# A layer norm's division and its shift moved from VectorE into TensorE's transposing products, and one tile's squares taken by halves

## The chip, the cores and the metric

The kernel runs on one core of a Trainium2 chip. The metric is the time of one execution in microseconds (us), and lower is better. The engines are named as in the profile: PE is TensorE (PEld its weight loads), DVE is VectorE, ACT is ScalarE, POOL is GpSimd, SP is SyncE, which here only issues DMAs.

## The reference, cut to what matters

Two transformer blocks run one after the other over 256 rows of 1024 floats. The change lies in the second block, between its attention and its feed-forward part:

```
def layer_norm(x, g, b):
    mu = jnp.mean(x, axis=-1, keepdims=True)
    var = jnp.mean(jnp.square(x - mu), axis=-1, keepdims=True)
    return (x - mu) * lax.rsqrt(var + LN_EPS) * g + b

def second_block(x, ...):
    mix = token_mixer(x, w_in, b_forget, rel_bias, w_out)        # ends in y @ w_out
    x = layer_norm(DEEPNORM_ALPHA * x + mix, ln1_g, ln1_b)       # the norm that is changed
    ffn = conv_ffn(x, w_up, conv_w, conv_b, w_down)              # begins with x @ w_up
    return layer_norm(DEEPNORM_ALPHA * x + ffn, ln2_g, ln2_b)
```

The norm is thus wanted twice: turned round (features on the partitions) as the input of the product with `w_up`, and multiplied by alpha, with rows on the partitions, for the sum behind the feed-forward part.

## The kernel before, in words

The 256 rows are two tiles (`tt` 0 and 1) of 128 rows on the partitions, and the 1024 features of a row are handled in two halves of 512. Every engine has its own program, written out by hand in one order, and engines wait for each other by semaphores; `wait_ge(made, ...)` waits for a step of DVE, `acted` of ACT, `done` of PE.

The stage around the change, with the lines of the profile:

1. The second output projection `out2` (L2223) adds the groups `("mix2", tt, half)` in four PSUM banks. The last of them to be ready is tile 1's second half.
2. For each tile DVE adds the projection to `xt` and sums the rows (`row_sum`, L1573, by halves), makes minus the mean (`row_mean`, L1581), and subtracts it and multiplies by the gain (`row_centre`, L1586) into `xg[4]`.
3. ACT squares the centred rows and sums them (`centred_squares`, L962), and takes the root (`row_root`, L632). DVE takes the reciprocal (`row_rstd`, L1129) and then writes the normed rows by halves, `xg * rstd + shift` (`row_normed`, L1595), into `xt`.
4. PE turns each half of a tile in four products with the identity (`turned_x4`, L2106), one PSUM bank a half. A product of two float32 operands stands in the trace as two MATMUL instructions, so a half has 8.
5. ACT rounds what was turned to the high part `h_r` (L853), DVE makes the low part, the rest (`turned_low`, L1446), half 0 of both tiles first.
6. PE begins the `up` products (L1703). Their first group of eight steps over the features (k = 0 to 7, three instructions each) reads half 0 of both tiles in its first four steps and half 1 in its last four.
7. Behind the low parts DVE multiplies `xt` by alpha (`x4_again`, L1602), then splits weights for `up` (L1021). The sum behind `down` reads that `xt` much later.

`row_diagonal` (L1137), which earlier norms use, writes a diagonal matrix with the reciprocals of one tile's roots; `turned_x` (L2096) turns rows by a product with it, so that turning and dividing are one product. The DMA queue of SP loads the gain and shift rows of this norm (`ln1`, L535) spread over all partitions, between two loads of `up` weights.

Of the kernel before, what the change touches and what calls it, by code (L numbers as in the profile page):

```python
# [8 lines left out]
F32 = mybir.dt.float32  # L9
# [6 lines left out]
P = 128  # L16
# [218 lines left out]
def build(nc, x_in, c_in, consts, bands_in, bmask_in, cols, relb, rows, w_ada, w_in, w_pool, w_br, w_out, w_q, keysT, uv, w_in2, w_f2,  # L235
          w_out2, w_up, w_down, out, sums):
    with ExitStack() as ctx:
# [146 lines left out]
        HALF = [slice(0, 512), slice(512, 1024)]  # L384
        by_rstd = [prob[:, 3, z * P:(z + 1) * P] for z in range(2)]

        def col(n, tt, what):

            c = 48 + 8 * tt + ("first", "sum", "squares", "part", "root", "rstd", "rstd alpha").index(what)
            return mx[:, c:c + 1]  # L390

# [8 lines left out]
        half_loaded = {n: Mark(sem(f"s_half{n[0]}{n[1]}"), 16) for n in (("ada", 0), ("ada", 2), ("in", 0), ("ada", 1), ("in", 1), ("ada", 3), ("in2", 2))}  # L400
        once = {n: Mark(sem("s_" + n), 16) for n in ("ct", "ct2", "cl", "x", "c", "bands", "wp", "wf", "rb", "bk", "gf", "g1", "b1", "g2", "b2")}
        arrived_in = {b: Mark(sem(f"s_rows{b[0]}{b[1]}"), 16) for b in bufs}
# [65 lines left out]
        def sync(e):  # L468
# [58 lines left out]
            for n in range(N_FIRST + 1, len(CHUNKS)):  # L527
                load(n)
                if CHUNKS[n][0:2] == ("in2", 3):
                    e.dma_start(util[:, 0:3072], relb).then_inc(*once["rb"].put(0))  # L530
                    e.dma_start(bmask, bmask_in).then_inc(*once["bk"].put(0))
                if CHUNKS[n][0:2] == ("up", 1):
                    sp.wait_ge(done, ("heads", 2, 7))
                    for z, name in enumerate(("g1", "b1")):
                        e.dma_start(ln1[z], rows[1 + z:2 + z, :].broadcast_to([P, D])).then_inc(*once[name].put(0))  # L535
                if CHUNKS[n][0:2] == ("up", 4):
# [48 lines left out]
        def scalar(e):  # L585
# [41 lines left out]
            def row_root(n, tt):  # L627
                if n in (2, 3):
# [3 lines left out]
                e.activation(col(n, tt, "root"), col(n, tt, "squares"), ACT.Sqrt,  # L632
                             bias=col(n, tt, "part") if n in (2, 3) else K("eps" if n == 1 else "eps5"), scale=1.0 / D).then_inc(*acted.put(("root", n, tt)))

# [323 lines left out]
            def centred_squares(n, tt):  # L958
# [4 lines left out]
                             accum_out=col(n, tt, "squares")).then_inc(*acted.put(("row squares", n, tt, 1)))  # L963

            sqrt_table(46)
# [48 lines left out]
        def vector(e):  # L1014
# [116 lines left out]
            def row_diagonal(n, tt):  # L1131
# [7 lines left out]
                if n == 3:  # L1139
                    e.tensor_scalar(col(n, tt, "rstd alpha"), col(n, tt, "rstd"), ALPHA, None, ALU.mult).then_inc(  # L1140
                        *made.put(("row rstd alpha", n, tt)))

# [445 lines left out]

            def row_normed(tt):

                row_rstd(4, tt)
                dve.wait_ge(made, ("row rstd", 4, tt))
                dve.wait_ge(made, ("row gain", 4, tt))
                for half in range(2):
                    e.scalar_tensor_tensor(xt[:, tt, HALF[half]], xg[4][:, tt, HALF[half]], col(4, tt, "rstd"),  # L1595
                                           ln1[1][:, HALF[half]], ALU.mult, ALU.add).then_inc(
                        *made.put(("row normed", 4, tt, half)))
# [18 lines left out]
            row_mean(4, 0)  # L1616
            row_centre(4, 0, ln1[0])
            row_sum(4, 1, "mix2", (0,), (made, ("x3", 1)))
            row_normed(0)
            row_sum(4, 1, "mix2", (1,))  # L1620
            row_mean(4, 1)
            row_centre(4, 1, ln1[0])
            row_normed(1)
            for half in range(2):
                for tt in range(2):
                    turned_low(4, h_r, lo_r, tt, half)
            for tt in range(2):
                x4_again(tt)
# [49 lines left out]
        def tensor(e):  # L1678
# [772 lines left out]
```

## Time and profile before

| | |
|---|---|
| median of 3 runs | 1154.97 us (1154.26 to 1155.44) |
| the profiled execution | 1154.77 us, its span 1153.0 us |
| busy: PE, DVE, ACT, POOL | 1033.9, 804.4, 549.0, 299.9 us |
| stage from the last output product to the first `up` product | about 952.6 to 959.5 us of the span |
| `up` products | 959.5 to 1084.7 us |
| `down` products and the last norm | 1084.7 to 1153.0 us |

The span is the time between the first and the last instruction of the profiled execution; 1.77 us of the execution's own time lie outside it. Busy time of PE is modelled from the starts of its instructions, so the step from one start to the next tells more of its pace than the length of one instruction.

### The profile page before, as it was taken

The page shows a single profiled execution, that of the slowest core. Times are in us where ns is not written, and L with a number is a line of the kernel's source. Part 1 is how long each engine was busy: PE and PEld are TensorE (multiplying, and loading weights), DVE is VectorE, ACT ScalarE, POOL GpSimd, SP SyncE. Part 2 cuts the span into 40 slices and gives each one's busy share as a digit, 9 for nine tenths or more (in the row PEclk, how much of TensorE's full clock was granted, in tenths as well). Part 3 has the DMA queues.
Part 4 walks back from the last instruction along what each step waited for, and adds up shares of the span by engine and source line. Part 5 has one row for each costly group of instructions (what it writes and reads, how often), then busy time and mean ns, then how long its engine had stood idle before and what let it go on. Part 6 is the DMA issues. An engine that isn't in the chain of part 4 may idle for free.

```text
span 1153.0 us, 13442 instructions
## 1 busy us (share of the span) xinstructions
PE 1033.9 (90%) x4830; PEld 675.9 (59%) x4830; DVE 804.4 (70%) x1680; ACT 549.0 (48%) x1303; POOL 299.9 (26%) x262
## 2 busy tenths in 40 slices
PE   6999999999999987886768888788799999999997
PEld 3798987644344333432323433333299978999986
DVE  6787886777676776878877655545476878887843
ACT  3465733433334332336876742222455666565631
POOL 0000002545345533455454454454000000000000
PEclk9999999999999998998998898899999999999999
DMA  9988697999999999999999999999875344545440
GB/s 378 423 354 323 249 387 288 397 422 421 422 421 420 422 421 422 420 422 422 422 422 420 422 422 421 421 422 422 360 333 202 129 182 167 195 188 188 178 146 37
DMA packets 48338, 390.08 MB, mean 338 GB/s; under 512 B 5514, under 2 KB 6034, under 8 KB 7316
## 3 DMA queue, kind: packets, MB, share of 16 engines
q0 software_dynamic: 37040, 269.51, 56.4%
q1 hardware_dynamic: 11236, 119.77, 26.4%
q8 instruction: 35, 0.57, 0.2%
q14 instruction: 27, 0.22, 0.1%
HBM read 388.20 MB, written 1.06 MB: 338 GB/s over the span
## 4 chain that ended last, share of the span: by engine, by line
PE 56%; DMA 32%; DVE 6%; ACT 5%; issue 2%; POOL 0%; SPq 0%; DVEq 0%; ACTq 0%
DMA ring<-in_uv,idx 29%; PE ps L1703 17%; PE ps L2135 10%; PE ps L2116 7%; PE ps L2295 5%; PE ps L1728 2%; PE ps L1884 2%; PE ps L1991 2%; PE ps L2223 2%; DMA ring<-in_w_ada 1%; DMA ring<-in_w_in 1%; DVE ring L1493 1%; DVE ring L1032 1%; ACT prob L882 1%; PE ps L1783 1%
## 5 line engine op out<-in xcount | busy, mean ns | idle before, releaser
L571 POOL DMA_INDIRECT ring<-in_uv,idx x247 | 287.9, 1166 | 317.8 <-PE ps L2135 149.8
L2116 PE MATMUL ps<-ring,probT 128*128 128x512 f32 x480 | 233.0, 642 | 59.7 <-ACT probT L888 59.7
L2135 PE MATMUL ps<-ring,probT 128*128 128x512 f32 x508 | 238.8, 606 | 32.1 <-ACT probT L888 32.1
L1493 DVE CUSTOM_DVE_ANT_0 ring<-h2t,ring 128x1024 f32<-128x1024 f32 x127 | 154.4, 1221 | 89.8 <-DMA ring<-in_uv,idx 89.4
L2116 PEld LDWEIGHTS ps<-ring,probT 128*128 128x128 f32 x480 | 95.3, 204 | 196.8 <-issue 109.9
L1703 PE MATMUL ps<-util_r,ring_r 128*128 128x256 f32 x1120 | 192.8, 282 | 0.3 <-ACT util L601 0.3
L2135 PEld LDWEIGHTS ps<-ring,probT 128*128 128x128 f32 x508 | 92.6, 192 | 154.6 <-issue 93.5
L1021 DVE TENSOR_TENSOR ring_r<-ring,ring_r 128x1024 fp32r<-128x1024 f32 (+1 forms) x134 | 155.5, 1203 | 35.1 <-ACT ring_r L597 35.1
L878 ACT ACTIVATE prob<-prob 128x2 f32<-128x2 f32 (+2 forms) x98 | 20.0, 204 | 316.4 <-DVE prob L1493 206.3
L1703 PEld LDWEIGHTS ps<-util_r,ring_r 128*128 128x128 f32 x1120 | 158.1, 188 | 1.3 <-issue 0.7
L597 ACT ACTIVATE ring_r<-ring 128x1024 fp32r<-128x1024 f32 (+1 forms) x134 | 132.0, 1039 | 38.0 <-PE ps L2295 19.1
L1457 DVE CUSTOM_DVE_ANT_0 ring<-h2t,ring 128x1024 f32<-128x1024 f32 x60 | 73.7, 1228 | 75.0 <-DMA ring<-in_uv,idx 75.0
L1703 PE MATMUL ps<-h_r,ring_r 128*128 128x256 f32 x704 | 125.2, 281 | 0.6 <-DVE util_r L1446 0.6
L1703 PEld LDWEIGHTS ps<-h_r,ring_r 128*128 128x128 f32 x704 | 108.1, 188 | 0.8 <-issue 0.8
L1491 DVE TENSOR_TENSOR ring<-h2t,ring 128x1024 f32<-128x1024 f32 x60 | 71.9, 1220 | 38.0 <-DMA ring<-in_uv,idx 37.9
L888 ACT ACTIVATE probT<-ct,prob 128x128 f32<-128x128 f32 x256 | 84.2, 387 | 0.3
L872 ACT ACTIVATE ring<-ring 128x1024 f32<-128x1024 f32 x60 | 63.2, 1053 | 35.8 <-DVE ring L1491 35.5
L882 ACT ACTIVATE prob<-prob 128x1 f32<-128x1 f32 x256 | 58.3, 285 | 3.2
L571 POOL DMA_INDIRECT area<-in_uv,idx x7 | 8.7, 1239 | 188.7 <-DVE h2t L1320 182.4
L1032 DVE CUSTOM_DVE_ANT_0 ring<-h2t,ring 128x1024 f32<-128x1024 f32 x44 | 51.5, 1220 | 4.1 <-DMA ring<-in_w_ada 3.7
L2295 PE MATMUL ps<-ring_r,util_r 128*128 128x512 f32 x176 | 50.1, 395 | 0.0
L1728 PE MATMUL ps<-ring_r,util_r 128*128 128x256 f32 x336 | 40.7, 280 | 0.0
(301 smaller groups left out, 1184.6 us busy)
## 6 DMA issues: line engine op xcount, KB each, us to landing
ring<-in_w_in SPq DMA_DIRECT2D x11, 2048.0 KB, 13.9
ring<-in_w_up SPq DMA_DIRECT2D x11, 2048.0 KB, 7.9
ring<-in_w_ada SPq DMA_DIRECT2D x7, 2048.0 KB, 9.2
ring<-in_w_down SPq DMA_DIRECT2D x6, 2048.0 KB, 7.9
ring<-in_w_ada SPq DMA_DIRECT2D x8, 1024.0 KB, 14.1
ring<-in_w_out SPq DMA_DIRECT2D x4, 2048.0 KB, 9.3
ring<-in_w_q SPq DMA_DIRECT2D x3, 2048.0 KB, 12.6
ring<-in_w_in SPq DMA_DIRECT2D x4, 1024.0 KB, 10.0
```

What stands on the lines that cost most here:

```text
L571: e.indirect_dma_start(out=row_buf[n], out_offset=None, in_=uv, in_offset=bass.IndirectOffsetOnAxis(ap=idx[:, tt, k:k + 1], axis=0)).then_inc(
L597: e.activation(hi, w, ACT.Copy).then_inc(*high.put(q))
L882: e.activation(wt[:, tt, k:k + 1], wt[:, tt, k:k + 1], ACT.Copy, scale=gw[:, tt, k:k + 1]).then_inc(*acted.put(("weight", 128 * tt + k)))
L888: e.activation(diag[:, n % DIAGS, :], ident, ACT.Copy, scale=wt[:, tt, n % 128:n % 128 + 1]).then_inc(*diagonals.put(n))
L1021: e.tensor_tensor(lo, w, hi.bitcast(F32), ALU.subtract).then_inc(*low.put(q))
L1457: e.tensor_tensor_reduce(u, h2t[:, 1, :], u, 1.0, 0.0, ALU.mult, ALU.add, av[:, 1, at:at + 1]).then_inc(made.sem, made.step)
L1491: e.tensor_tensor(u, h2t[:, tt, :], u, ALU.mult).then_inc(*made.put(("dot", n)))
L1493: e.tensor_tensor_reduce(u, h2t[:, tt, :], u, 1.0, 0.0, ALU.mult, ALU.add, av[:, tt, at:at + 1]).then_inc(*made.put(("dot", n)))
L1703: ins = e.matmul(o[:, jj * T:(jj + 1) * T], w[:, k, :], r[:, k, :], start=(k == 0 and n == 0), stop=(k == KD - 1 and n == 2))
L2116: ins = e.matmul(acc[half][:, :], diag[:, (first + j) % DIAGS, :], row_buf[first + j][:, D + half * 512:D + (half + 1) * 512], start=False ...
L2135: ins = e.matmul(acc[half][:, :], diag[:, n % DIAGS, :], row_buf[n][:, D + half * 512:D + (half + 1) * 512], start=(k == 0), stop=(k == 127))
L2295: ins = e.matmul(ps[where["down", tt, half]][:, :], h[:, k, tile[tt]], w[:, 0, HALF[half]], start=(k == 0 and n == 0), stop=(k == KF - 1 a ...
```

## The change

Four things are done, all in the norm behind the second output projection.

- DVE no longer writes normed rows (`row_normed` is gone). It makes `row_diagonal` for each tile, and `row_centre` is done by halves. PE turns `xg[4]` by the diagonal instead of `xt` by the identity.
- The shift is added by PE too: a DMA brings the shift row as 4 partitions of two rows of 128 floats (`shift`, in the space of `idx`), and before the four turning products of each half one product of 4 partitions x 128 columns of weights with 4 x 512 moving elements, a 4 x 4 identity of which each element is repeated 128 times, writes the shift into the whole bank. The turning products then add to it.
- Tile 1's squares are taken by halves on ACT: the first half about the mean of that half alone (`first_mean`), as soon as that half is there, the second half too, and DVE corrects the sum by four operations on one column (`part_about_first`).
- `x4_again` is computed anew from `xg[4]`, with the root's reciprocal times alpha (`row_alpha`) and the shift times alpha, which ACT multiplies beforehand.

The core of the diff, shortened:

```diff
+            act.wait_ge(once["b1"], 0)
+            e.activation(ln1[1], ln1[1], ACT.Copy, scale=ALPHA).then_inc(*acted.put("shift alpha"))
             centred_squares(4, 0)
             row_root(4, 0)
-            centred_squares(4, 1)
+            for half in range(2):
+                squares_by_half(4, half)
             row_root(4, 1)
...
             def x4_again(tt):
 
-                dve.wait_ge(done, ("turned x", 4, tt, 1))
-                e.tensor_scalar(xt[:, tt, :], xt[:, tt, :], ALPHA, None, ALU.mult).then_inc(*made.put(("x4", tt)))
+                dve.wait_ge(acted, "shift alpha")
+                dve.wait_ge(made, ("row rstd alpha", 4, tt))
+                dve.wait_ge(made, ("row gain", 4, tt, 1))
+                e.scalar_tensor_tensor(xt[:, tt, :], xg[4][:, tt, :], col(4, tt, "rstd alpha"), ln1[1], ALU.mult,
+                                       ALU.add).then_inc(*made.put(("x4", tt)))
...
             row_mean(4, 0)
-            row_centre(4, 0, ln1[0])
+            for half in range(2):
+                row_centre_half(4, 0, half, ln1[0])
             row_sum(4, 1, "mix2", (0,), (made, ("x3", 1)))
-            row_normed(0)
+            first_mean(4)
+            row_diagonal(4, 0)
             row_sum(4, 1, "mix2", (1,))
+            part_about_first(4)
             row_mean(4, 1)
-            row_centre(4, 1, ln1[0])
-            row_normed(1)
+            row_centre_half(4, 1, 0, ln1[0])
+            row_diagonal(4, 1)
+            row_centre_half(4, 1, 1, ln1[0])
...
             def turned_x4(tt):
+                pe.wait_ge(once["shift"], 0)
                 for half in range(2):
-                    pe.wait_ge(made, ("row normed", 4, tt, half))
                     o = group(("turned x", 4, tt, half))
+                    e.matmul(o[:, :].rearrange("p (k t) -> p k t", k=4), shift[:, half, :], shift_of, start=True, stop=False)
+                    pe.wait_ge(made, ("row diagonal", 4, tt))
+                    pe.wait_ge(made, ("row gain", 4, tt, half))
                     for k in range(4):
                         c = 512 * half + k * P
-                        ins = e.matmul(o[:, k * P:(k + 1) * P], xt[:, tt, c:c + P], ident, start=True, stop=True)
+                        ins = e.matmul(o[:, k * P:(k + 1) * P], xg[4][:, tt, c:c + P], by_rstd[tt], start=False, stop=k == 3)
```

How the change moves instructions on PE, from the end of the output projection to the first `up` product (`ps` is a PSUM bank, `ct` the constants with the identity, `idx` the space of the shift, `prob` that of the diagonals, `area` that of `xg[4]`). Before:

```order
L2223 MATMUL ps3<-ring_r,h_r 128x512
L2106 MATMUL ps0<-ct,x_sb 128x128 [waits s_dve]
L2106 MATMUL ps0<-ct,x_sb 128x128 x3
L2106 MATMUL ps2<-ct,x_sb 128x128 [waits s_dve]
L2106 MATMUL ps2<-ct,x_sb 128x128 x3
L2106 MATMUL ps1<-ct,x_sb 128x128 [waits s_dve]
L2106 MATMUL ps1<-ct,x_sb 128x128 x3
L2106 MATMUL ps4<-ct,x_sb 128x128 [waits s_dve]
L2106 MATMUL ps4<-ct,x_sb 128x128 x3
L1703 MATMUL ps5<-h_r,ring_r 128x256 [waits s_dve,s_low]
```

Now, in the same place:

```order
L2275 MATMUL ps3<-ring_r,h_r 128x512
L2153 MATMUL ps0<-ct,idx 128x512 [waits s_shift]
L2158 MATMUL ps0<-prob,area 128x128 [waits s_dve]
L2158 MATMUL ps0<-prob,area 128x128 x3
L2153 MATMUL ps2<-ct,idx 128x512
L2158 MATMUL ps2<-prob,area 128x128 x4
L2153 MATMUL ps1<-ct,idx 128x512
L2158 MATMUL ps1<-prob,area 128x128 [waits s_dve]
L2158 MATMUL ps1<-prob,area 128x128 x3
L2153 MATMUL ps4<-ct,idx 128x512
L2158 MATMUL ps4<-prob,area 128x128 [waits s_dve]
L2158 MATMUL ps4<-prob,area 128x128 x3
```

One product of 512 columns now stands ahead of the four products of each half, and the first of these waits for no step of DVE in this stage. Each row counts a float32 product once.

DVE from tile 1's second row sum to the first low part (`x_sb` is `xt`, `mx` holds columns of one number a row, `util_r` the low parts). Before:

```order
L1573 ISA x_sb,mx<-x_sb,ps3,mx 128x512 [waits s_pe]
L1573 ISA mx 128x1
L1581 TENSOR_SCALAR mx<-mx 128x1 [waits s_dve]
L1586 SCALAR_TENSOR_TENSOR area<-x_sb,mx,area 128x1024 [waits s_dve]
L1129 RECIPROCAL mx<-mx 128x1 [waits s_act]
L1595 SCALAR_TENSOR_TENSOR x_sb<-area,mx 128x512 [waits s_dve]
L1595 SCALAR_TENSOR_TENSOR x_sb<-area,mx 128x512
L1446 TENSOR_TENSOR util_r<-ps0,h_r 128x4x128 [waits s_act]
```

Now:

```order
L1598 ISA x_sb,mx<-x_sb,ps3,mx 128x512 [waits s_pe]
L1598 ISA mx 128x1
L1630 SCALAR_TENSOR_TENSOR mx<-mx 128x1 [waits s_dve]
L1633 TENSOR_SCALAR mx<-mx,ct 128x1 [waits s_act]
L1635 TENSOR_SCALAR mx<-mx 128x1 [waits s_dve]
L1637 SCALAR_TENSOR_TENSOR mx<-mx 128x1 [waits s_dve]
L1606 TENSOR_SCALAR mx<-mx 128x1
L1617 SCALAR_TENSOR_TENSOR area<-x_sb,mx,area 128x512 [waits s_dve]
L1150 RECIPROCAL mx<-mx 128x1 [waits s_act]
L1158 TENSOR_SCALAR prob<-ct,mx 128x128 [waits s_dve]
L1617 SCALAR_TENSOR_TENSOR area<-x_sb,mx,area 128x512
L1471 TENSOR_TENSOR util_r<-ps0,h_r 128x4x128 [waits s_act]
```

The two wide passes behind the reciprocal are gone and a diagonal of 128 x 128 stands there; ahead of it are four more operations on one column.

## Rows read from the trace of the kernel before

**Rows 1.** The page: share of the span by engine, and the chain that ended last.

```profile
span 1153.0 us, 13442 instructions
PE 1033.9 (90%) x4830; PEld 675.9 (59%) x4830; DVE 804.4 (70%) x1680; ACT 549.0 (48%) x1303; POOL 299.9 (26%) x262
PE 56%; DMA 32%; DVE 6%; ACT 5%; issue 2%; POOL 0%; SPq 0%; DVEq 0%; ACTq 0%
```

**Rows 2.** The chain from 952 us on: start, length, what; released step by step.

```profile
955.79 0.17 DVE mx L1129
955.97 0.03 issue
955.99 0.76 DVE x_sb L1595
956.75 0.04 issue
956.80 1.17 PE ps L2106 x8
957.97 0.02 issue
957.99 0.61 ACT h_r L853
958.60 0.02 issue
958.62 0.70 DVE util_r L1446
959.33 0.14 issue
959.46 125.20 PE ps L1703 x1056
```

**Rows 3.** Busy time by stretches: engines in the page's order, granted clock, DMA share, GB/s.

```profile
952.60:959.50 6.90, 4.24 (x34) 3.79 (x33) 5.86 (x12) 3.72 (x8) 0.00 (x0) 1.00 0.83 302
959.50:1084.70 125.20, 125.20 (x1057) 125.19 (x1058) 102.45 (x154) 77.84 (x110) 0.00 (x0) 1.00 0.49 177
```

**Rows 4.** PE in order of time: start, length, line, count, [idle before and its end].

```profile
952.40 0.39 PE L2223 MATMUL ps<-ring_r,h_r 128*128 128x512 f32 x1
952.70 2.05 PE L2106 MATMUL ps<-ct,x_sb 128*128 128x128 f32 x16
956.80 2.05 PE L2106 MATMUL ps<-ct,x_sb 128*128 128x128 f32 x16 [2.05 <-DVE x_sb L1595]
959.46 0.36 PE L1703 MATMUL ps<-h_r,ring_r 128*128 128x256 f32 x1 [0.61 <-DVE util_r L1446]
...
957.46 1.39 PE L2106 MATMUL ps<-ct,x_sb 128*128 128x128 f32 x11
...
L2106 PE MATMUL ps<-ct,x_sb x32: 275/275/377, 952.7 to 958.6; 128*128 128x128 f32 x32
...
952.16 0.40 PE L2223 MATMUL ps<-ring_r,h2t_r 128*128 128x512 f32 x1
```

**Rows 5.** PE elsewhere: float32 products of 512 columns in a row.

```profile
28.00 7.03 PE L1833 MATMUL ps<-ring,h_sb 128*128 128x512 f32 x16
...
L1833 PE MATMUL ps<-ring,h_sb x16: 592/592/592, 28.0 to 34.4; 128*128 128x512 f32 x16
```

**Rows 6.** PE around the only products of few rows among products of 128 rows.

```profile
495.26 1.12 PE L1814 MATMUL ps<-h_sb,ct 1*128 1x512 f32 x2
496.31 3.70 PE L2135 MATMUL ps<-ring,probT 128*128 128x512 f32 x8
499.94 1.12 PE L1814 MATMUL ps<-h_sb,ct 1*128 1x512 f32 x2
500.99 0.70 PE L2135 MATMUL ps<-ring,probT 128*128 128x512 f32 x1
```

**Rows 7.** DVE in order of time from the row sums to the `up` stage.

```profile
951.09 0.68 DVE L1573 CUSTOM_DVE_ANT_0 x_sb<-x_sb,ps 128x512 f32<-128x512 f32 x1
953.22 0.74 DVE L1573 CUSTOM_DVE_ANT_0 x_sb<-x_sb,ps,mx 128x512 f32<-128x512 f32 x1
954.00 0.15 DVE L1581 TENSOR_SCALAR mx<-mx 128x1 f32<-128x1 f32 x1
954.19 1.28 DVE L1586 SCALAR_TENSOR_TENSOR area<-x_sb,mx,area 128x1024 f32<-128x1024 f32 x1
955.99 1.41 DVE L1595 SCALAR_TENSOR_TENSOR x_sb<-area,mx 128x512 f32<-128x512 f32 x2
957.32 0.68 DVE L1446 TENSOR_TENSOR util_r<-ps,h_r 128x512 fp32r<-128x512 f32 x1
960.43 1.28 DVE L1602 TENSOR_SCALAR x_sb<-x_sb 128x1024 f32<-128x1024 f32 x2
961.63 2.35 DVE L1021 TENSOR_TENSOR ring_r<-ring,ring_r 128x1024 fp32r<-128x1024 f32 x2
966.47 1.65 DVE L1644 SCALAR_TENSOR_TENSOR prob<-ps,cl,prob 128x255 f32<-128x255 f32 x4 [2.50 <-ACT prob L985]
```

**Rows 8.** The diagonal of earlier norms (ns, least/median/most).

```profile
L1137 DVE TENSOR_SCALAR prob<-ct,mx x6: 286/287/289, 14.3 to 838.1; 128x128 f32<-128x128 f32 x6
```

**Rows 9.** ACT in order of time through the stage.

```profile
945.97 0.20 ACT L619 ACTIVATE mx<-ct 128x1 f32<-128x1 f32 x1
949.89 1.15 ACT L962 ACTIVATE prob<-x_sb,mx 128x1024 f32<-128x1024 f32 x1 [3.71 <-DVE mx L1581]
955.46 0.29 ACT L632 ACTIVATE mx<-mx,ct 128x1 f32<-128x1 f32 x1
958.89 0.60 ACT L853 ACTIVATE h_r<-ps 128x512 fp32r<-128x512 f32 x1 [0.30 <-PE ps L2106]
```

**Rows 10.** The DMA queue of SP, and DMA issues with us to landing.

```profile
923.43 0.91 SPq L535 DMA_DIRECT2D area<-in_rows  x2
939.03 0.33 SPq L485 DMA_DIRECT2D ring<-in_w_up  x1
...
area<-in_rows SPq DMA_DIRECT2D x2, 512.0 KB, 10.1
```

More of the change, by code:

```diff
@@ L385, in build, with near @@
         by_rstd = [prob[:, 3, z * P:(z + 1) * P] for z in range(2)]
+        shift = idx[0:4, :, :].bitcast(F32)
+        shift_of = ident[0:4, 0:4].unsqueeze(2).broadcast_to([4, 4, P])
         def col(n, tt, what):
             c = 48 + 8 * tt + ("first", "sum", "squares", "part", "root", "rstd", "rstd alpha").index(what)
+            return mx[:, c:c + 1]
+        def near(what):
+            c = 32 + ("first mean", "apart", "by apart").index(what)
             return mx[:, c:c + 1]
@@ L535, in sync @@
                         e.dma_start(ln1[z], rows[1 + z:2 + z, :].broadcast_to([P, D])).then_inc(*once[name].put(0))
+                    e.dma_start(shift, rows[2:3, :].rearrange("o (h k f) -> (o k) h f", h=2, k=4)).then_inc(
+                        *once["shift"].put(0))
                 if CHUNKS[n][0:2] == ("up", 4):
@@ L632, in row_root @@
                 e.activation(col(n, tt, "root"), col(n, tt, "squares"), ACT.Sqrt,
-                             bias=col(n, tt, "part") if n in (2, 3) else K("eps" if n == 1 else "eps5"), scale=1.0 / D).then_inc(*acted.put(("root", n, tt)))
+                             bias=col(n, tt, "part") if n in (2, 3) or (n, tt) == (4, 1) else K("eps" if n == 1 else "eps5"),
+                             scale=1.0 / D).then_inc(*acted.put(("root", n, tt)))
             for half in range(2):
@@ L963, in centred_squares, with squares_by_half @@
                              accum_out=col(n, tt, "squares")).then_inc(*acted.put(("row squares", n, tt, 1)))
+            def squares_by_half(n, half):
+                act.wait_ge(made, ("row sum", n, 1, half))
+                act.wait_ge(made, ("first mean", n))
+                e.activation(junk[5][:, HALF[half]], xt[:, 1, HALF[half]], ACT.Square, bias=near("first mean"),
+                             accum_out=col(n, 1, "squares" if half else "part")).then_inc(
+                    *acted.put(("row squares", n, 1, half)))
             sqrt_table(46)
+            act.wait_ge(once["b1"], 0)
+            e.activation(ln1[1], ln1[1], ACT.Copy, scale=ALPHA).then_inc(*acted.put("shift alpha"))
             centred_squares(4, 0)
             row_root(4, 0)
-            centred_squares(4, 1)
+            for half in range(2):
+                squares_by_half(4, half)
             row_root(4, 1)
@@ L1139, in row_diagonal, with row_alpha @@
                 if n == 3:
-                    e.tensor_scalar(col(n, tt, "rstd alpha"), col(n, tt, "rstd"), ALPHA, None, ALU.mult).then_inc(
-                        *made.put(("row rstd alpha", n, tt)))
+                    row_alpha(n, tt)
+            def row_alpha(n, tt):
+                e.tensor_scalar(col(n, tt, "rstd alpha"), col(n, tt, "rstd"), ALPHA, None, ALU.mult).then_inc(
+                    *made.put(("row rstd alpha", n, tt)))
             for half in range(2):
@@ L1587, in row_centre @@
                     *made.put(("row gain", n, tt)))
[L1589 to L1597, printed above, removed]
@@ L1599, in x4_again, with row_centre_half @@
-            def x4_again(tt):
-                dve.wait_ge(done, ("turned x", 4, tt, 1))
-                e.tensor_scalar(xt[:, tt, :], xt[:, tt, :], ALPHA, None, ALU.mult).then_inc(*made.put(("x4", tt)))
+            def row_centre_half(n, tt, half, g):
+                dve.wait_ge(made, ("row mean", n, tt))
+                e.scalar_tensor_tensor(xg[n][:, tt, HALF[half]], xt[:, tt, HALF[half]], col(n, tt, "sum"), g[:, HALF[half]],
+                                       ALU.add, ALU.mult).then_inc(*made.put(("row gain", n, tt, half)))
@@ new lines, in first_mean, with part_about_first @@
+            def first_mean(n):
+                dve.wait_ge(made, ("row sum", n, 1, 0))
+                e.tensor_scalar(near("first mean"), col(n, 1, "first"), -2.0 / D, None, ALU.mult).then_inc(
+                    *made.put(("first mean", n)))
+            def part_about_first(n):
+                part, apart, by = col(n, 1, "part"), near("apart"), near("by apart")
+                dve.wait_ge(made, ("row sum", n, 1, 1))
+                e.scalar_tensor_tensor(apart, col(n, 1, "first"), -2.0, col(n, 1, "sum"), ALU.mult, ALU.add).then_inc(
+                    *made.put(("apart", n)))
+                dve.wait_ge(acted, ("row squares", n, 1, 0))
+                e.tensor_scalar(part, part, 1.0 / D, K("eps5"), ALU.mult, ALU.add).then_inc(*made.put(("first part", n)))
+                dve.wait_ge(made, ("apart", n))
+                e.tensor_scalar(by, apart, -1.0 / (D * D), None, ALU.mult).then_inc(*made.put(("by apart", n)))
+                dve.wait_ge(made, ("by apart", n))
+                e.scalar_tensor_tensor(part, apart, by, part, ALU.mult, ALU.add).then_inc(*made.put(("row part", n, 1)))
@@ L1626, in vector @@
                     turned_low(4, h_r, lo_r, tt, half)
+            for tt in range(2):
+                row_alpha(4, tt)
             for tt in range(2):
```

4 lines of the change are left out of this document (2 added, 2 removed).

## The prediction

> **What bounds the kernel now.** I read the page first: PE is busy for 90% of the span and holds the largest share of the chain that ended last [rows 1]. That is an average, so the next view is the chain from the changed stage on [rows 2]. It shows a stretch in which PE is not the bound: the reciprocal on DVE at 955.79, a wide pass, eight turning products, ACT's rounding, DVE's low part, and then, from 959.46, 1056 `up` products in 125.20 us, 0.1186 us each, without a gap. The table by stretches says the same [rows 3]: PE works 4.24 of 6.90 us between 952.6 and 959.5, then 125.20 of 125.20. So whatever moves the first `up` product moves the end by the same amount; nothing later can take it up, because PE never waits there. The granted clock is 1.00 in the stage, that is 2.4 GHz [rows 3].
>
> PE's own order of time shows how much room the stage has [rows 4]. The last output product starts at 952.40; products of that kind follow each other every 0.23 us (952.16 to 952.40), so PE is free at 952.63. It turns tile 0, waits 2.05 us for tile 1's normed rows, turns tile 1, and waits 0.61 us for the low part. PE thus stands idle for 2.66 us of the 6.83 between 952.63 and 959.46. This is the room into which the change puts new PE work.
>
> **DVE and ACT, part by part.** Tile 1's path gets shorter up to PE. The row sum started at 953.22, behind two wide passes of tile 0 [rows 7]; now only small operations and a diagonal of 0.29 us [rows 8] stand there, and it waits for PE's last output product (952.40 plus its length of 0.39) instead, so about 952.9. The sum takes 0.74. Behind it come three corrections that wait for each other, at 0.19 each as the mean's step does (954.00 to 954.19): 954.25. ACT's second half of the squares lies beside them: half of 1.15 [rows 9], plus about 0.2 to read the sum out, ends near 954.5, the root of 0.29 near 954.8. DVE meanwhile takes the mean and one centred half (half of 1.41 for two [rows 7]) until about 955.15, then the reciprocal (0.17 and 0.03 [rows 2]) and the diagonal: 955.65. Before, the first normed half was there at 956.75 [rows 2]. DVE and ACT deliver tile 1 some 1.1 us earlier.
>
> ACT's multiplication of the shift by alpha, 128 x 1024, costs about as much as its squares, 1.15, and lies in the 3.71 us in which ACT waits ahead of 949.89 [rows 9]; the shift rows were issued at 923.43 and take 10.1 us to land [rows 10]. The new DMA stands behind them in SP's queue; the `up` load behind it starts at 939.03 [rows 10], far later than a third issue of half of 0.91 us would end. Both cost nothing. Without that cover ACT's copy would cost its 1.15.
>
> `x4_again` becomes dearer: two passes of three operands, 1.28 each like the centring, in place of 1.28 for two [rows 7], and two multiplications of one column, some 1.6 us in all. They stand behind the last low part, and behind them is the weight split of 961.63, then DVE waits 2.50 us for ACT [rows 7]. That idle time takes the 1.6 us; the sums behind `down` need the result only after 1084.7 [rows 3]. I cost it at nothing; without that cover, the wait for the next `up` weights could at most grow by 1.6.
>
> **PE's own work.** This is the term that decides. Four float32 products of 512 columns are added, two instructions each. Sixteen such instructions take 7.03 us, the last of them 0.592 [rows 5], so the step is (7.03 - 0.592) / 15 = 0.429 and a product 0.858. The turning products number 32 instructions as before, now with the diagonal as moving operand; eleven of them take 1.39, of which the last one's own length is 0.275, so the step is (1.39 - 0.275) / 10 = 0.1115 [rows 4]. The shift's weights have 4 partitions, the turning products' 128, and PE changes between them eight times: into and out of each of the four shift products. The trace has one place like it [rows 6]: two instructions of 1 row between products of 128 rows take 1.05 us from start to start (495.26 to 496.31), not 0.858, and the eight behind them 3.63 (496.31 to 499.94), not 3.43. So each change of the number of rows costs 0.19 to 0.20, also at the second place (499.94 to 500.99). No row shows 4 rows, nor a change beside products of 128 columns; the bounds are 0 (a change that loads under way) and 0.3 (a whole last product, 0.275, left to end). I take 0.195, since the nearest row has both directions of it.
>
> The Trainium skill, "TensorEngine Tiling (Array Packing)", section Key Properties, says that a change of the tiling mode drains TensorE, without a price. The trace agrees, with 0.195 us a change at its one place. If 4 rows and 128 rows counted as one mode the sum below would be 0.4; by the rule it stays at 2.0.
>
> From 952.63: 4 x 0.858 = 3.43, 32 x 0.1115 = 3.57, 8 x 0.195 = 1.56, together 8.56. PE is through at 961.19 and has not waited: it comes to tile 1's first turning product at 952.63 + 3 x 0.858 + 16 x 0.1115 + 5 x 0.195 = 957.96, 2.3 us after the diagonal. The earlier rows from DVE buy nothing. Half 0 of both tiles is rounded long before 961.19, so `up` starts there, 1.73 later than at 959.46. Its first four steps, 12 products, last 1.42; the fifth needs the low part of what PE turned last. That product starts at 961.08 and ends 0.275 later, 961.35; then 0.04 to ACT (958.85 to 958.89), ACT 0.60 [rows 4, 9], 0.02, DVE 0.68 [rows 7], 0.14 to PE [rows 2]: 962.83. PE is there at 962.61 and waits 0.22. Before, there was no such wait. Sum: 1.73 + 0.22 = 1.95, about 2.0 us later.
>
> The span becomes 1155.0. The profiled execution took 1154.77 with a span of 1153.0, so it would become 1156.75; the median of the runs is 0.20 above it, so I predict 1157.0. A measurement of this kernel can tell about 0.2%, 2.3 us, from no change: 1157.3 is the line, and the forecast lies just under it.
>
> **The rivals.**
> - **The changes of rows are free.** Weights of 4 rows may be loaded under a running product, as those of 128 are. Against it stand two places of two [rows 6]. It would take 1.56 off: 0.4 later, 1155.4. Chance 10%.
> - **The shift fits into PE's idle time.** If the four-row products with their changes cost less than (959.46 - 952.63 - 3.57) / 4 = 0.8 us each, PE is no longer late, and well below that the 1.1 us of DVE and ACT come through: 1153.9. For it speak PE's 2.66 idle microseconds [rows 4] and that 4 rows are little arithmetic; against it, that one row took 1.05 with its changes and no less than 0.858 without [rows 6]. Chance 6%. This is the side on which it ends faster, though by 0.1% only.
> - **The repeated element is slow to read, or the clock falls.** The moving operand repeats each element 128 times in place; no row shows a product fed like that. At half the pace it adds 4 x 0.858 = 3.4: 1160.4. A clock of 1.2 GHz for a few microseconds of the stage would add as much; against it, the clock stayed at 1.00 with PE idle for more than a third of this stretch [rows 3]. Chance 10%.
>
> **How the numbers follow.** The forecast holds 74%. Its own range is 1155.9 to 1158.3: the changes at 0.1 to 0.3 each, and some 0.4 for the runs' scatter. About three tenths of it lie over the line of 1157.3, so slower has 0.22 and the slow operand's 0.10 less a little: 0.31. Faster by over 0.2% needs more than 2.3 us, twice what the second rival gives: 0.01. The rest, 0.68, is no difference that can be told. The range 1155.1 to 1158.4 holds the forecast and the first rival and leaves out the other two, 16%.
>
> **What would show it.** Right: in the profile after, PE has no wait from the last output product to the `up` products, eight intervals of about 1.05 and 1.09 us alternate there, and the first `up` product starts near 961.2, with a short wait at its thirteenth; tile 1's diagonal is there some 2 us before PE comes to it; the `up` stretch still lasts about 125.2. Wrong: PE waits for the diagonal (the second rival), the steps of the shift products are longer than 0.43 (the third), or the change of rows leaves no trace in the steps (the first). A wait inside the `up` stretch would mean that DVE's dearer `x4_again` was not covered.

## The result, and the profile after

The changed kernel takes 1157.08 us in the median (1156.39 to 1162.41, 12 runs), the kernel before 1154.89 (1153.54 to 1156.58, 12 runs): a ratio of 1.0027, 95% interval 1.0016 to 1.0037. It is slower by about 2.2 us. The twelve runs fall into two groups: seven lie between 1156.39 and 1157.39 (median 1156.63), five between 1158.80 and 1162.41. The profiled execution, 1156.39 with a span of 1154.6, is the lowest of the first group, so it shows what the stage costs when nothing else happens.

The chain that ended last, of the changed kernel, from the last output product on (start, length, what). It answers to [rows 2]:

```profile
951.98 0.47 PE ps L2275 x2
952.45 1.05 PE ps L2153 x2
953.50 1.09 PE ps L2158 x8
...
959.92 1.10 PE ps L2158 x8
...
961.04 0.61 ACT h_r L863
...
961.67 0.69 DVE util_r L1471
962.37 0.13 DVE mx L1165 x2
...
962.51 123.78 PE ps L1752 x1044
```

Before, the stretch up to the `up` products ran over DVE and ACT; now it runs over PE. Shift products of 1.05 us and turning products of 1.09 us alternate four times, then come 12 `up` instructions that the chain leaves out, the thirteenth waits for the low part of the last half, and it and the 1043 behind it follow without a gap. PE's own order of time, in the same stretch, answers to [rows 4] (start, length, line, operation, output and inputs, count):

```profile
952.05 0.39 PE L2275 MATMUL ps<-ring_r,h_r 128*128 128x512 f32 x1
952.38 1.12 PE L2153 MATMUL ps<-ct,idx 4*128 4x512 f32 x2
...
957.71 1.16 PE L2158 MATMUL ps<-prob,area 128*128 128x128 f32 x8
...
960.76 0.37 PE L1752 MATMUL ps<-h_r,ring_r 128*128 128x256 f32 x1
```

No wait stands ahead of any of these rows: from the last output product to the first `up` product PE takes 8.71 us (952.05 to 960.76), where it took 7.06 before, 2.66 of them idle [rows 4]. DVE's order of time, which answers to [rows 7], shows that its part did come forward:

```profile
952.48 0.75 DVE L1598 CUSTOM_DVE_ANT_0 x_sb<-x_sb,ps,mx 128x512 f32<-128x512 f32 x1 [0.34 <-PE ps L2275]
954.64 0.16 DVE L1150 RECIPROCAL mx<-mx 128x1 f32<-128x1 f32 x1
954.84 0.28 DVE L1158 TENSOR_SCALAR prob<-ct,mx 128x128 f32<-128x128 f32 x1
```

Tile 1's diagonal is there at 955.12 (954.84 and 0.28), and PE comes to its first use at 957.71 (above): it lies ready for 2.6 us. The stretches of [rows 3] now read (length, then busy time and instructions of PE, weight loads, DVE, ACT and POOL, the granted clock, the DMA share and GB/s):

```profile
952.60:961.40 8.80, 8.80 (x45) 5.40 (x45) 4.93 (x14) 3.31 (x8) 0.00 (x0) 1.00 0.65 240
961.40:1086.60 125.20, 125.11 (x1056) 124.84 (x1054) 103.80 (x155) 78.31 (x111) 0.00 (x0) 1.00 0.48 177
```

PE is busy for all of the stage, and the granted clock is 1.00, which is 2.4 GHz. Among the `up` products PE waits once: the thirteenth starts 0.37 us behind the twelfth (962.14 to 962.51), where such steps are 0.12, so it comes 0.25 late. From the first `up` product to the end of the chain's last piece above it is 125.53 (960.76 to 1086.29), 0.33 more than the 125.20 of before [rows 2]. The work ahead of the stage ended 0.35 us earlier in this profile (the last output product starts at 952.05, not 952.40), so the span grew by 1.6 only.

### The profile page after: what moved, and what is told of

Same layout as the page of the kernel before. It is cut to its first block, busy times and chain, and to the rows that moved or that the text cites. A ratio compares the mean times of both kernels' runs of the same rounds, so it can differ in the third digit from the quotient of the medians.

```text
span 1154.6 us, 13471 instructions
## 1 busy us (share of the span) xinstructions
PE 1037.2 (90%) x4838; PEld 676.5 (59%) x4838; DVE 804.8 (70%) x1687; ACT 550.5 (48%) x1306; POOL 301.1 (26%) x262
## 3 DMA queue, kind: packets, MB, share of 16 engines
HBM read 388.21 MB, written 1.06 MB: 337 GB/s over the span
## 4 chain that ended last, share of the span: by engine, by line
PE 55%; DMA 32%; DVE 6%; ACT 4%; issue 2%; POOL 0%; SPq 0%; DVEq 0%; ACTq 0%
DMA ring<-in_uv,idx 29%; PE ps L1752 17%; PE ps L2187 9%; PE ps L2168 6%; PE ps L2347 5%; PE ps L1777 2%; DMA ring<-in_w_ada 2%; PE ps L1933 2%; PE ps L2275 2%; PE ps L2040 2%; DVE ring L1053 1%; PE ps L1988 1%; DVE ring L1518 1%; ACT prob L892 1%; ACT ring L882 1%
```

## The experiments

What tells most in each is the time from the start of the last output product to the start of the first `up` product, since what stands behind it is nearly the same: only where the four shift products alternate with the turning products does the thirteenth `up` product come 0.25 late as well. I call it the stage: 7.06 us before, 8.71 with the change. Each kernel is the changed kernel with the edit that is shown, shortened, unless the text says otherwise.

### What a change of the number of rows costs

The first experiment feeds the shift through all 128 partitions: the rows of `idx` behind the fourth meet only zeros of the identity. PE does the same number of steps, and the number of rows never changes.

```diff
-        shift_of = ident[0:4, 0:4].unsqueeze(2).broadcast_to([4, 4, P])
+        shift_rows = idx[:, :, :].bitcast(F32)
+        shift_of = ident[:, 0:4].unsqueeze(2).broadcast_to([P, 4, P])
...
-                    e.matmul(o[:, :].rearrange("p (k t) -> p k t", k=4), shift[:, half, :], shift_of, start=True, stop=False)
+                    e.matmul(o[:, :].rearrange("p (k t) -> p k t", k=4), shift_rows[:, half, :], shift_of, start=True, stop=False)
```

> The changed kernel, but the shift product takes all 128 partitions (the identity is zero in the rows behind the fourth), so that no product changes the number of rows. Result unchanged. Theory (PE is the bound of the stage, and eight changes of the number of rows cost 0.195 us each): from the last output product's start to the first up product's 8.71 - 1.56 = about 7.15 us, the span about 1.5 shorter than with the change, 0.4 longer than before. Rival (the shift products cost what they cost by their 512 columns or by reading one element 128 times, whatever their rows): the steps into and out of them stay as they are, 8.7 us, and the time is that of the changed kernel.

The median is 1154.91 (11 runs), that of before in the same session 1155.30: ratio 1.0001 (0.9992 to 1.0010). PE's order of time:

```profile
951.91 0.39 PE L2276 MATMUL ps<-ring_r,h_r 128*128 128x512 f32 x1
952.14 1.02 PE L2154 MATMUL ps<-ct,idx 128*128 128x512 f32 x2
953.00 1.05 PE L2159 MATMUL ps<-prob,area 128*128 128x128 f32 x8
953.89 1.02 PE L2154 MATMUL ps<-ct,idx 128*128 128x512 f32 x2
...
959.07 0.37 PE L1753 MATMUL ps<-h_r,ring_r 128*128 128x256 f32 x1
```

The steps are 0.86 and 0.89 instead of 1.05 and 1.09, and the stage is 7.16 us, 1.55 shorter than with the change. Divided by eight that is 0.194 a change. The shift products themselves run at 0.43 an instruction, the pace of the float32 products of [rows 5], 0.429, so the repeated element of the moving operand costs nothing here.

Two more kernels ask whether the price hangs on the four rows: the shift over 64 and over 32 partitions (`idx[0:64, :, :]` with `ident[0:64, 0:4]`, and the same with 32).

> The changed kernel with the shift products over 64 partitions (zeros in the identity behind the fourth). Result unchanged. Theory (any change of the number of rows costs its 0.2 us, the fall of the clock comes from products of few rows): in an execution without a fall the first up product starts about 8.7 us after the last output product, as with 4 rows, the time some 1.6 over that with 128 rows; executions 1 to 6 us above that are rarer or gone. Rival (what costs is the number of rows left idle, not the change): between the 7.16 of 128 rows and 8.71.

> The same over 32 partitions. Result unchanged. Theory: the changes of rows as with 4 and with 64, about 8.7 us to the first up product without a fall of the clock; if 32 rows are as few as 4 to whatever lowers the clock, executions 1 to 6 us above the fastest come as often as with the change.

With 64 rows the median is 1156.16 (11 runs, highest 1157.07), ratio 1.0012 (1.0003 to 1.0021) to a before of 1154.88; with 32 rows 1156.38 (11 runs, highest 1157.96), ratio 1.0013 (1.0004 to 1.0022). The stage is 8.72 (951.75 to 960.47) and 8.71 (951.77 to 960.48), that of the change. PE with 64 rows:

```profile
952.07 1.12 PE L2154 MATMUL ps<-ct,idx 64*128 64x512 f32 x2
953.13 1.16 PE L2159 MATMUL ps<-prob,area 128*128 128x128 f32 x8
```

The step is 1.06, as with four rows. So 4, 32 and 64 rows pay the same price against 128. What differs is the spread of the runs: neither of the two has a run over 1158. They ran on another chip than the repeated runs of four rows below, though, and no four-row kernel was run beside them.

### Leaving the shift out

> The changed kernel without the four shift products: the shift is left out of the input of the up products (it is still added for the last norm). Theory: PE waits for tile 1's diagonal again, and DVE's and ACT's 1.1 us come through: 7.06 - 1.1 = about 6.0 us from the last output product to the first up product, 1.1 faster than before, ratio 0.999, and 3.1 faster than with the change. Rival (the loss lies in what DVE and ACT do more, the dearer second pass for the last norm or the corrections): no more than the 3.4 us of the shift products' own time are taken from PE's busy time, and the up products begin no earlier than before.

The edit drops the shift product, so that the input of `up` lacks the shift; the rest is computed as before.

```diff
-                    e.matmul(o[:, :].rearrange("p (k t) -> p k t", k=4), shift[:, half, :], shift_of, start=True, stop=False)
...
-                        ins = e.matmul(o[:, k * P:(k + 1) * P], xg[4][:, tt, c:c + P], by_rstd[tt], start=False, stop=k == 3)
+                        ins = e.matmul(o[:, k * P:(k + 1) * P], xg[4][:, tt, c:c + P], by_rstd[tt], start=True, stop=True)
```

The median is 1153.58 (11 runs), ratio 0.9984 (0.9975 to 0.9993). PE's order of time, with the wait ahead of a row in brackets:

```profile
953.32 0.39 PE L2274 MATMUL ps<-ring_r,h_r 128*128 128x512 f32 x1
953.55 2.02 PE L2157 MATMUL ps<-prob,area 128*128 128x128 f32 x16
956.44 2.05 PE L2157 MATMUL ps<-prob,area 128*128 128x128 f32 x16 [0.86 <-DVE prob L1158]
959.11 0.36 PE L1752 MATMUL ps<-h_r,ring_r 128*128 128x256 f32 x1 [0.61 <-DVE util_r L1471]
```

The stage is 5.79, where about 6.0 was expected. PE waits again, for the diagonal and then for the low part. What DVE and ACT gain is real: tile 1's turning starts 3.12 after the last output product, where it started 4.40 after it before [rows 4]. The change spends that 1.28 and more on four shift products.

### The rows of the shift in one piece

The four shift products are issued one behind the other, ahead of all turning, so that the number of rows changes twice and not eight times.

```diff
...
             for tt in range(2):
+                for half in range(2):
+                    shift_x4(tt, half)
+            for tt in range(2):
                 turned_x4(tt)
```

> The changed kernel with all four shift products first and the turning products behind them, so that PE changes the number of rows twice instead of eight times. Result unchanged. Theory: 6 x 0.195 = 1.2 us less, 8.71 - 1.17 = about 7.5 us from the last output product to the first up product, still some 0.8 slower than before. Rival (each shift product costs 1.05 us by itself): 8.7 us as with the change.

The median is 1158.08 (7 runs), ratio 1.0022 (1.0011 to 1.0034). The stage was expected at 7.5 and took 10.04 (952.30 to 962.34). PE's order of time, and the table by stretches, with the granted clock ahead of the last two columns:

```profile
952.62 3.71 PE L2152 MATMUL ps<-ct,idx 4*128 4x512 f32 x8
956.26 5.47 PE L2161 MATMUL ps<-prob,area 128*128 128x128 f32 x32
962.34 0.36 PE L1752 MATMUL ps<-h_r,ring_r 128*128 128x256 f32 x1 [0.61 <-DVE util_r L1471]
```

```profile
952.60:956.20 3.60, 3.60 (x9) 1.40 (x8) 3.16 (x11) 1.42 (x5) 0.00 (x0) 1.00 0.69 209
957.00:960.30 3.30, 3.30 (x18) 3.30 (x18) 0.69 (x1) 1.19 (x2) 0.00 (x0) 0.50 0.70 298
```

Behind 3.6 us in which PE ran four-row products, without a gap, and 0.7 us of turning products at full pace, the granted clock falls to 0.50, that is 1.2 GHz, and the turning products go at half pace. To part the two effects, the same order was run with 128 rows:

> All four shift products first, as in the grouped run, but over 128 partitions. Result unchanged. If the clock fell there because the products had four rows: the granted clock stays 1.00, and the first up product starts 0.23 + 3.43 + 3.57 = about 7.2 us after the last output product, as with 128 rows in turn. If it fell because products that are almost all zeros, or that repeat one element, stand 3.4 us in a row: the clock falls again and the first up product starts after about 9 to 10 us.

The median is 1155.45 (11 runs, highest 1156.54), ratio 1.0003 (0.9994 to 1.0012). PE's order of time and the two stretches:

```profile
952.04 0.39 PE L2279 MATMUL ps<-ring_r,h_r 128*128 128x512 f32 x1
952.27 3.61 PE L2153 MATMUL ps<-ct,idx 128*128 128x512 f32 x8
955.72 3.73 PE L2162 MATMUL ps<-prob,area 128*128 128x128 f32 x32
960.06 0.36 PE L1753 MATMUL ps<-h_r,ring_r 128*128 128x256 f32 x1 [0.61 <-DVE util_r L1472]
```

```profile
952.20:955.80 3.60, 3.60 (x11) 1.62 (x10) 3.16 (x11) 1.56 (x5) 0.00 (x0) 1.00 0.70 191
955.80:960.00 4.20, 3.65 (x33) 3.46 (x31) 1.47 (x3) 2.30 (x5) 0.00 (x0) 1.00 0.82 339
```

The clock stays at 1.00. The stage is 8.02 and not 7.2, so my expectation missed here too: with all turning products in one piece behind the shift products, from 955.72 on, the rounding of tile 1's first half and its low part end late, and `up` waits 0.61 for them. In the interleaved order that half is rounded while PE still turns. The grouped four-row kernel adds up from this: 8.02, two changes at 0.195, and half of the 3.41 us (956.98 to 960.39) at half clock, 1.7, are 10.1; 10.04 was measured. The two groups also tell the price of a four-row product from that of a change: eight four-row instructions in a row take 3.64 (952.62 to 956.26), only 0.19 more than with 128 rows (952.27 to 955.72, 3.45), while alternating already two of them lose 0.19 (1.05 against 0.86). So it is the change that costs, not the product of few rows.

### The same kernel again, and its clock

Since grouping four-row products lowers the clock, the five high runs of the changed kernel could be the same thing. So it was run again, unedited.

> The changed kernel once more, beside the others on one chip. Single executions of it lay up to 6 us over its fastest. Theory (the four-row products can make the clock fall in some executions, as they did when grouped): times near 1156.5 and others 1 to 4 us above, in one look perhaps a granted clock of 0.5 for some microseconds in the stage. Rival (a property of the chip of that run, whatever the kernel): the kernels beside it scatter as far.

The median is 1158.61 (1157.06 to 1162.78, 9 runs), ratio 1.0039 (1.0025 to 1.0053) to a before of 1155.11. The two kernels without four-row products that ran beside it (128 rows grouped, and the mixed one below) scatter by less than 2 us each, the kernel before by 3.2 (1153.80 to 1156.98, 32 runs). The profiled execution, 1158.61, is the middle one of the nine:

```profile
953.03 0.39 PE L2275 MATMUL ps<-ring_r,h_r 128*128 128x512 f32 x1
962.38 0.56 PE L1752 MATMUL ps<-h_r,ring_r 128*128 128x256 f32 x1
```

```profile
953.35:961.05 7.70, 7.70 (x35) 4.29 (x35) 4.30 (x13) 3.19 (x8) 0.00 (x0) 1.00 0.76 274
961.05:964.46 3.41, 3.41 (x18) 3.41 (x18) 1.81 (x6) 1.69 (x3) 0.00 (x0) 0.50 0.00 0
964.46:970.00 5.54, 5.54 (x48) 5.54 (x48) 4.48 (x4) 1.52 (x3) 0.00 (x0) 1.00 0.00 0
```

PE is busy in every part of these stretches, and yet the granted clock is 0.50 from 961.05 to 964.46, behind four-row and turning products that followed each other without a gap. The span, 1156.8, is 2.2 over that of the first profile, but 0.98 of it lies ahead of the stage (the last output product starts at 953.03, not 952.05). So the fall costs about 1.2, less than the 1.7 that half the pace for 3.41 would make, in part because the thirteenth `up` product no longer waits. The Trainium skill, "TensorE: Matmul & The Clock Gate", section Part 1, ties the lower level to a PE that was idle before. Here PE had not been idle, so for this case the measurement decides: with products of four rows the clock can fall under a PE that always has work. In the ten profiles without such a fall, the kernel before and the first profile of the change among them, the granted clock is 1.00 all the way from 800 to 1145 us; the three that show one there all have products of four rows.

### One tile's squares whole again

This one undoes the fourth part of the change: tile 1's squares are taken in one piece, without the correction on DVE.

```diff
...
-            for half in range(2):
-                squares_by_half(4, half)
+            centred_squares(4, 1)
...
-            first_mean(4)
...
-            part_about_first(4)
```

> The changed kernel with tile 1's squares taken whole again, behind the mean, and without the corrections. Result unchanged. Theory (PE comes to tile 1's diagonal 2.3 us after it is there): the root comes some 0.5 us later or earlier, nobody waits for it, the first up product starts 8.7 us after the last output product as with the change. Rival (DVE's path to the diagonal sets the stage): the time moves by that half microsecond.

The median is 1158.53 (1156.08 to 1163.34, 12 runs), ratio 1.0032 (1.0021 to 1.0044). Tile 1's reciprocal starts 3.01 us after the last output product (951.63 to 954.64), where it starts 2.59 after it with the change, so the halves do bring 0.4 us; but PE comes to the diagonal only 5.66 after that product (952.05 to 957.71), and nobody waits. The lowest run, 1156.08, is close to that of the change, 1156.39. The profiled execution, 1161.95, was one with a long fall of the clock, and its stage of 13.26 (951.63 to 964.89) therefore tells nothing of the squares:

```profile
955.20:968.80 13.60, 13.60 (x47) 10.14 (x47) 5.38 (x9) 3.68 (x5) 0.00 (x0) 0.50 0.26 112
```

### No shift on PE, norming by halves

Here DVE norms by halves, and PE turns normed rows with the identity, as before the change; the squares by halves stay.

```diff
...
+            def row_normed_half(tt, half):
...
+                e.scalar_tensor_tensor(xt[:, tt, HALF[half]], xg[4][:, tt, HALF[half]], col(4, tt, "rstd"),
+                                       ln1[1][:, HALF[half]], ALU.mult, ALU.add).then_inc(
...
             row_centre_half(4, 1, 0, ln1[0])
-            row_diagonal(4, 1)
+            row_rstd(4, 1)
+            row_normed_half(1, 0)
             row_centre_half(4, 1, 1, ln1[0])
+            row_normed_half(1, 1)
```

> One part of the change alone: tile 1's squares by halves, and the centring and the norming by halves too, but dividing and shifting stay on DVE and PE turns with the identity as before. Theory (the stage sets the end, and its path goes through DVE as long as PE is not loaded): the first normed half of tile 1 comes 0.6 us earlier, the up products begin about 0.6 earlier than before, ratio 0.9995. Rival (the halves cost DVE more small operations than they save): the up products begin as before or later.

The median is 1155.01 (11 runs), ratio 0.9999 (0.9990 to 1.0008). PE's order of time:

```profile
952.04 0.39 PE L2275 MATMUL ps<-ring_r,h_r 128*128 128x512 f32 x1
952.65 2.05 PE L2158 MATMUL ps<-ct,x_sb 128*128 128x128 f32 x16 [0.22 <-DVE x_sb L1639]
956.33 1.16 PE L2158 MATMUL ps<-ct,x_sb 128*128 128x128 f32 x8 [1.63 <-DVE x_sb L1639]
957.78 1.16 PE L2158 MATMUL ps<-ct,x_sb 128*128 128x128 f32 x8 [0.29 <-DVE x_sb L1639]
959.07 0.36 PE L1755 MATMUL ps<-h_r,ring_r 128*128 128x256 f32 x1
```

The stage is 7.03, as before the change and not the 0.6 shorter that was hoped for. The first half of tile 1 comes 0.1 us earlier, 4.29 after the last output product against 4.40 [rows 4], and the second half then waits for DVE's normed rows. What the halves of the squares bring, the norming of tile 0 on DVE takes again: it stands ahead of tile 1's second row sum, which starts 1.13 after the last output product, where it starts 0.43 after it with the change (952.05 to 952.48):

```profile
953.17 0.74 DVE L1594 CUSTOM_DVE_ANT_0 x_sb<-x_sb,ps,mx 128x512 f32<-128x512 f32 x1
```

### Each tile where there is room

Before the change PE idles for 2.05 us ahead of tile 1's turning [rows 4], while DVE works for it. So tile 0 is divided and shifted by PE, with two shift products of 128 rows in one piece, and tile 1 is normed by DVE, by halves. ACT multiplies the shift by alpha only behind that, and DVE's `x4_again` of tile 1 is that of before.

```diff
...
+                if tt == 0:
+                    for half in range(2):
+                        e.matmul(groups[half][:, :].rearrange("p (k t) -> p k t", k=4), shift_rows[:, half, :], shift_of,
+                                 start=True, stop=False)
...
             row_centre_half(4, 1, 0, ln1[0])
-            row_diagonal(4, 1)
+            row_rstd(4, 1)
+            row_normed_half(1, 0)
             row_centre_half(4, 1, 1, ln1[0])
+            row_normed_half(1, 1)
```

> A version meant to beat both kernels. Tile 0 is divided and shifted by PE, with its two shift products first and over 128 partitions, in the time in which PE waits anyway; tile 1 is normed by DVE by halves, its squares taken by halves, and turned with the identity. Result unchanged. Theory (PE's serial work decides only where it exceeds the wait for tile 1): PE is through with tile 0 about 3.7 us after the last output product's start, tile 1's first normed half is there at about 3.5, and the first up product starts after about 6.4, 0.65 earlier than before (7.06); ratio 0.9994. Rival (any shift product on PE delays tile 1, or the halves cost DVE as much as they save): 7.0 us or more.

The median is 1153.92 (1153.12 to 1155.03, 11 runs), ratio 0.9987 (0.9979 to 0.9996) to the before of 1155.11 beside it. PE's order of time:

```profile
952.43 0.39 PE L2300 MATMUL ps<-ring_r,h_r 128*128 128x512 f32 x1
952.66 1.89 PE L2169 MATMUL ps<-ct,idx 128*128 128x512 f32 x4
954.38 1.95 PE L2181 MATMUL ps<-prob,area 128*128 128x128 f32 x16
956.17 1.06 PE L2183 MATMUL ps<-ct,x_sb 128*128 128x128 f32 x8
957.48 1.16 PE L2183 MATMUL ps<-ct,x_sb 128*128 128x128 f32 x8 [0.25 <-DVE x_sb L1657]
958.76 0.36 PE L1767 MATMUL ps<-h_r,ring_r 128*128 128x256 f32 x1
```

The stage is 6.33, 0.73 shorter than before; PE's wait is down to 0.25. By the median it is 1.2 us faster than the kernel before, of which the stage explains 0.73; that is little, but the interval excludes no change.

### The cover of `x4_again`

On the 128-row kernel each pass of `x4_again` is done three times, so that DVE has some 5.2 us more behind the last low part.

```diff
...
+                for again in range(3):
+                    e.scalar_tensor_tensor(xt[:, tt, :], xg[4][:, tt, :], col(4, tt, "rstd alpha"), ln1[1], ALU.mult,
+                                           ALU.add).then_inc(*made.put(("x4", tt) if again == 2 else ("x4", tt, again)))
...
```

> The 128-row version with each of the two passes that compute the rows for the last norm done three times, some 5.1 us more of DVE behind the last low part. Result unchanged. Theory (the waits of DVE in the up stage cover it): the up products take the same 125.2 us without a gap, the time is that of the 128-row version, about as before. Rival (DVE's dearer pass is what delays the up stage): gaps among the up products, up to 5 us slower, which would put the 1.2 us that the change itself adds there among its costs.

The median is 1154.70 (11 runs), ratio 0.9999 (0.9990 to 1.0008). DVE's order of time and the `up` stretch:

```profile
961.29 7.77 DVE L1646 SCALAR_TENSOR_TENSOR x_sb<-area,mx 128x1024 f32<-128x1024 f32 x6
968.97 2.35 DVE L1043 TENSOR_TENSOR ring_r<-ring,ring_r 128x1024 fp32r<-128x1024 f32 x2
```

```profile
961.00:1086.00 125.00, 124.91 (x1052) 124.56 (x1051) 108.21 (x159) 77.50 (x111) 0.00 (x0) 1.00 0.49 177
```

Six passes take 7.77, 1.295 each, and the weight split behind them starts 5 us later, but PE is busy for 124.91 of 125.00 and the time is that of the 128-row kernel. The two dearer passes are covered, and so are six.

## Why the prediction was right, and where it was not

**The sum of the stage was right.** From the last output product to the thirteenth `up` product, the first that waits, it was 8.56 before (952.40 to 960.96, by the starts in PE's order of time) and should have been 1.95 more; it is 10.46 after (952.05 to 962.51). That is 1.9, and the wait ahead of the thirteenth product is there, 0.25 where 0.22 was forecast. The first `up` product stands at 960.76, and with the 0.35 by which the work ahead ended earlier at 961.11; 961.19 was forecast.

**Its terms, each by a run.** The change of rows, taken as 0.195 from a place with one row in a different stage [rows 6], measured 0.194 by the 128-row kernel, and the same with 32 and 64 rows; neither bound, 0 or 0.3, was near. The Trainium skill, "TensorEngine Tiling (Array Packing)", section Key Properties, says that a change of the tiling mode drains TensorE; the runs agree as far as 4, 32 and 64 rows against 128 go. The step of the shift products, 0.43, is that of the 128-row kernel. The diagonal was forecast 2.3 us ahead of PE and is 2.6 ahead. DVE and ACT were to deliver 1.1 earlier (its step to 954.25 adds up to 954.21, which changes nothing), and without the shift products tile 1's turning starts 1.28 earlier. ACT's multiplication of the shift by alpha lies at 945.74, over 6 us ahead of the last output product, and `x4_again` has cover for three times its work; DVE's wait for ACT behind the weight split, 2.50 before [rows 7], is 0.89 after. Halves of squares buy nothing here, since PE comes to the diagonal late in any case.

**The rivals.** That the changes of rows are free, and that the shift fits into PE's idle time, both fell with the same measurement: a four-row product takes 1.05 with one change and 1.25 with both, over the 0.8 from which PE would not be late. Even without the changes, in the 128-row kernel, the stage is 7.16, and the shift takes all that DVE and ACT gave. That the repeated element is slow to read fell too.

**What was wrong** is the step on the clock. The prediction held against a fall to 1.2 GHz that "the clock stayed at 1.00 with PE idle for more than a third of this stretch", and gave it, with the slow operand, one chance in ten. It thus took PE's idle time for what decides, and asked only about work that takes the place of idleness. The runs show a fall of the clock under a PE that is busy throughout, in the profiled executions of the grouped kernel, of the change when run again, and of the change with whole squares. Over all kernels with interleaved four-row products (12, 9 and 12 runs) 16 of 33 runs lie over 1158.5; with 32 and 64 rows none of 22 lies over 1158, and with 128 rows none over 1156.6. The kernel before itself scatters by up to 3.9 (1153.82 to 1157.67 in 29 runs), so a short fall can't be told by a time; nine of the 33 lie over 1161.6, though, and the mean granted clock of these is 0.966 to 0.972, that of the other 24 is 0.971 to 0.982. A fall like that of the third profile, 13.65 us at half clock in some 1160, lowers the mean by 0.006. So the prediction's 1157.0 beside the measured 1157.08 agrees better than it should: the lower group lies at 1156.63, 1.7 over before, and the high runs lift the median by the other 0.45. That part of the agreement is luck. When the kernel was run again, the median was 1158.61, above the range.

**What stays open.** The five high runs of the first twelve were not profiled. For the two over 1162 the mean granted clock, 0.971 and 0.967 against 0.972 to 0.980 in the other ten, speaks for a long fall; for the three from 1158.80 to 1160.04 a fall is inferred from the profiles and the counts alone. Why the clock falls in some executions of one kernel and not in others is not shown. That 32 and 64 rows are free of it is not shown either: each has one profile, without a fall, and no run of four rows beside it on that chip, and its times lie too close together for a long fall but not for a short one.

## What to carry to other kernels

Work that is moved to an engine with idle time must be counted with its surcharges: PE had 2.66 us free, and four products of 0.86 with a turn of 0.19 on either side overran it. Feed a product of few rows through all 128 partitions, with zeros against the rows that don't count: it costs no more steps, saves the changes, and kept the clock up here. And where two engines have room at different times, split the tiles between them and not the kind of work: tile 0 on PE and tile 1 on DVE was, of the arrangements that leave nothing out, the one that beat the kernel before.

## What the hardware showed that I had not expected

With products of four rows, back to back in one kernel and alternating with 128-row products in the others, the granted clock fell to 0.50, for 3.4 us in two profiles and for 13.65 us (955.19 to 968.84) in a third, though PE ran without a gap ahead of it; in a fourth profile, that of the change above, it stayed at 1.00. The price is at most half of the stretch: about 1.2 us in the repeated run, and 5.9 in the third profile, whose span of 1160.1 is 5.5 over that of the change although its last output product starts 0.42 earlier. Four profiles with the shift product over 128 partitions show no such fall, nor does the one each with 32 and 64 rows. And a change between 32 or 64 rows and 128 costs as much as one between 4 and 128: 0.19 us.
